# Where the causal mask of the attention scores is added: on TensorE before the score products, or on VectorE after them

## What is computed

```python
        s_own = jnp.einsum('bhqd,bhkd->bhqk', qf, k_own) * scale
        s_own = jnp.where(k_pos[None, :] <= q_pos[:, None], s_own, NEG)
        p = jax.nn.softmax(jnp.concatenate([s_sel, s_own], axis=-1), axis=-1)
```

## Time and profile before

| what | value |
|---|---|
| time, median of 3 runs | 826.17 us (826.13 to 826.72) |
| time of the profiled execution | 826.71 us |
| its span | 825.0 us |
| mean granted TensorE clock | 0.999 of 2.4 GHz |
| TensorE products busy | 815.7 us |
| VectorE busy | 612.4 us |
| ScalarE busy | 460.1 us |
| GpSimd busy | 153.2 us |

### The profile page before, as it was taken

One profiled execution on the slowest core, in us unless ns is written; L12 is line 12 of the kernel. 1 busy time (PEld: TensorE's weight loads), 2 busy tenths in 40 slices (PEclk: granted clock), 3 DMA queues, 4 the chain that ended last, 5 costly groups with the idle time before them and its releaser, 6 DMA issues.

```text
span 825.0 us, 12737 instructions
## 1 busy us (share of the span) xinstructions
PE 815.7 (99%) x4962; PEld 719.4 (87%) x4962; DVE 612.4 (74%) x734; ACT 460.1 (56%) x628; POOL 153.2 (19%) x146
## 2 busy tenths in 40 slices
PE   8999999999999999999999999999999999999997
PEld 8999888888989999999999988878899888888885
DVE  6899888977786766565787898888687767565664
ACT  6757687534664464545465577755355554445544
POOL 2407754082000000000000385523300000000000
PEclk9999999999999999999999999999999999999999
DMA  9976545567545555645567565465645465646451
GB/s 299 284 240 193 163 162 187 216 205 218 174 154 179 182 199 184 223 153 204 158 209 247 166 215 170 153 216 166 214 161 174 153 205 169 223 167 200 158 177 52
DMA packets 103598, 156.17 MB, mean 189 GB/s; under 512 B 4081, under 2 KB 68899, under 8 KB 103553
## 3 DMA queue, kind: packets, MB, share of 16 engines
q1 hardware_dynamic: 102080, 153.50, 56.5%
q0 software_dynamic: 1296, 1.79, 0.8%
q10 hardware_dynamic: 176, 0.27, 0.1%
HBM read 152.39 MB, written 1.05 MB: 186 GB/s over the span
## 4 chain that ended last, share of the span: by engine, by line
PE 93%; DVE 2%; ACT 2%; DMA 1%; issue 1%; DVEq 0%; ACTq 0%
PE bank L1093 19%; PE bank L1095 10%; PE bank L1038 8%; PE bank L1040 8%; PE bank L1039 8%; PE bank L981 7%; PE bank L982 7%; PE bank L983 7%; PE bank L1069 5%; PE bank L1070 5%; PE bank L1068 5%; ACT w_hi L648 1%; DMA raw<-in_w_in 1%; DVE w_lo L1445 1%; PE bank L1178 1%
## 5 line engine op out<-in xcount | busy, mean ns | idle before, releaser
L1445 DVE TENSOR_TENSOR w_lo<-raw,w_hi 128x2048 fp32r<-128x2048 f32 x135 | 318.6, 2361 | 133.1 <-ACT w_hi L648 132.4
L648 ACT ACTIVATE w_hi<-raw 128x2048 fp32r<-128x2048 f32 (+3 forms) x146 | 264.4, 1818 | 128.9 <-PE bank L1040 55.6
L1093 PE MATMUL bank<-act,w_hi 128*128 128x512 f32 x704 | 247.6, 395 | 0.0
L1095 PE MATMUL bank<-act,w_lo 128*128 128x256 f32 x704 | 197.0, 280 | 0.0
L1093 PEld LDWEIGHTS bank<-act,w_hi 128*128 128x128 f32 x704 | 132.0, 187 | 30.2
L1095 PEld LDWEIGHTS bank<-act,w_lo 128*128 128x128 f32 x704 | 132.9, 189 | 0.4
L1038 PE MATMUL bank<-w_hi,act 128*128 128x512 f32 x288 | 114.3, 397 | 0.0
L1040 PE MATMUL bank<-w_hi,act 128*128 128x512 f32 x288 | 112.3, 390 | 0.0
L1039 PE MATMUL bank<-w_lo,act 128*128 128x512 f32 x288 | 112.1, 389 | 0.0
L648 ACT ACTIVATE qk<-bank 128x256 f32<-128x256 f32 (+1 forms) x96 | 37.5, 395 | 76.4 <-PE bank L1095 76.3
L981 PE MATMUL bank<-act,w_hi 128*128 128x256 f32 x256 | 73.3, 286 | 1.2 <-DVE w_lo L1785 1.0
(11 more groups left out here) (250 smaller groups left out, 1453.0 us busy)
## 6 DMA issues: line engine op xcount, KB each, us to landing
raw<-in_w_ffn_in SPq DMA_DIRECT2D x44, 1024.0 KB, 5.1
raw<-in_w_gate SPq DMA_DIRECT2D x32, 1024.0 KB, 5.5
raw<-in_w_ffn_out SPq DMA_DIRECT2D x22, 1024.0 KB, 5.0
raw<-in_w_in SPq DMA_DIRECT2D x18, 1024.0 KB, 6.1
raw<-in_w_o SPq DMA_DIRECT2D x8, 1024.0 KB, 5.1
raw<-in_w_proj_b SPq DMA_DIRECT2D x4, 1024.0 KB, 4.9
raw<-in_w_in SPq DMA_DIRECT2D x12, 256.0 KB, 6.2
gates<-qk SPq DMA_DIRECT2D x32, 64.0 KB, 4.8
```

The costliest lines, as they stand in the source:

```text
L648: return nc.scalar.activation(o, i, ACT.Copy)
L1093: nc.tensor.matmul(bank[b + f], hi[:, k, fs], act2[:, k, :, :].rearrange("p h s -> p (h s)"), start=(k == 0), stop=False, skip_group_check ...
L1095: last = nc.tensor.matmul(main(b)[:, f, :], lo[:, k, fs], act_hi[:, k, :], start=False, stop=(k == KT - 1), skip_group_check=True)
L1445: V.tensor_tensor(w_lo[slot][:, :], raw[slot][:, :], w_hi[slot][:, :].bitcast(F32), ALU.subtract)\
```

## The change

The mask moves from TensorE to VectorE. TensorE's four mask products per pair go, and with them `ident16` and its copy on GpSimd; the first score product of each bank now starts the accumulation. `causal` becomes fp32. VectorE, once it has the scores, adds the mask in place in both banks and both diagonal blocks in one operation (2 banks x 2 blocks x 128 columns = 512 elements per partition, both the input and the output in PSUM, the mask read from SBUF for each of the four blocks) and waits for it with `link` before the reductions.

```diff
-DVE_CHAIN_PER_LAYER = 66
+DVE_CHAIN_PER_LAYER = 70
...
-        causal = sb("causal", [P, P], BF16)
-        ident16 = sb("ident16", [P, P], BF16)
+        causal = sb("causal", [P, P])
...
             pool.wait_ge(pre_const, 5)
-            nc.gpsimd.tensor_copy(ident16[:, :], ident[:, :])
-
...
                         bank_wait(l, 4 + i, f"S{hp}")
-                        nc.tensor.matmul(bank[4 + i][:, 0:P], ident16[:, :], causal[:, :], start=True, stop=False,
-                                         skip_group_check=True)
-                        nc.tensor.matmul(bank[4 + i][:, 2 * P:3 * P], ident16[:, :], causal[:, :], start=False,
-                                         stop=False, skip_group_check=True)
-
                     for i in range(2):
                         h = slice(64 * i, 64 * i + 64)
-                        nc.tensor.matmul(bank[4 + i][:, 0:P], qk[h, hp, 0:P], qk[h, 4 + hp, 0:P], start=False,
+                        nc.tensor.matmul(bank[4 + i][:, 0:P], qk[h, hp, 0:P], qk[h, 4 + hp, 0:P], start=True,
                                          stop=False, skip_group_check=True)
...
                     dve.wait_ge(s_done, l * 2 * HP + 2 * hp + 2)
+                    own = banks[:, 4:6, :].rearrange("p b (q k) -> p b q k", q=2)[:, :, :, 0:P]
+                    link(l, V.tensor_tensor(own, own, causal[:, :].unsqueeze(1).unsqueeze(1).to_broadcast([P, 2, 2, P]),
+                                            ALU.add))
                     V.tensor_reduce(mx[:, 0:2], banks[:, 4:6, 0:P], AX.X, ALU.max)
```

## The result

The changed kernel takes 831.25 us (median of 4, 829.70 to 832.43) against 826.34 us (826.13 to 826.72) beside it: the ratio is 1.0058, with a 95% interval of 1.0046 to 1.0070. It is slower by 4.9 us, where 1.5 us were forecast and 829.5 was the top of the range. The profiled execution took 829.70 us, span 828.0, so 3.0 us more than the profile of before. The 4.9 us are the sum of three parts: 3.0 us are in the profile, 1.5 us more lie between this execution, the fastest of the four, and their median, and 0.4 us between the profiled execution of before (826.71) and the median of its kernel.

What follows compares the result with a forecast made beforehand. TensorE was taken as the bound, but with nothing to spare at pair 3's probabilities, fed by VectorE's chain. These come 0.75 us later per layer; two layers, +1.5 on 826.17, gave 827.7 us, range 825.9 to 829.5.

Steps and rivals of the forecast that it cites:

- The gain of 0.24 per pair: TensorE's stream: of 0.33 us for the mask products, 0.09 stays as turning price; 0.24 saved per pair, 1.9 us in all.
- The place where it is lost: TensorE's transposes of pair 3 at unit 21: it waits about 1.7 us per layer for ScalarE's scaling of the probabilities.
- The price of the mask operation: VectorE's added operation: 0.69 us plus 0.04 for `link`, 0.73 per pair.
- The rival of a dear write to PSUM: VectorE's mask operation costs up to 1.11 us because it writes PSUM; 829.4 us, chance 0.18.
- `nmx` of pair 3 held by GpSimd's third tap: VectorE's `nmx` at pair 3 starts behind GpSimd's tap, takes near 0.68 us and ends 0.75 later than before.
- The rival of 826.7: Pair 3's `nmx` gets in before GpSimd's tap, takes 0.17 and ends 0.24 later per layer; 826.7 us, chance 0.12.
- The sum, pair 2 and pair 3: Chain through VectorE and ScalarE: exponentials move by -0.13 us at pair 2, probabilities of pair 3 by +0.75 per layer.
- All that follows on VectorE to the gates of unit 16 is +0.25: After pair 1's reduction moves by 0.73 - 0.48, VectorE's following tasks up to these gates all come 0.25 us later.
- its weak place: GpSimd's taps meet other VectorE operations; each meeting moves the chain up to 0.4 us either way, spread 826.9 to 828.7.
- Granted clock still 1.00 in both waits: Sign expected in the profile after: clock stays at 1.00 during TensorE's two waits of 1.7 us at pair 3.
- The rival that the gain is kept: TensorE keeps all eight savings of 0.24 us, with no loss at pair 3; 824.3 us, chance 0.10.

Runs made afterwards that it cites:

- the filler: Changed kernel with 36 products of zeros on TensorE in place of idling before pair 3's probabilities; 829.91 us, ratio 1.0035 against the kernel before.

## Why the prediction was wrong

- *The gain of 0.24 per pair*: right (0.32 in place of 0.56; 0.93 for the four pairs of a layer, 0.96 forecast).
- *The place where it is lost*: right. The only new wait is pair 3's transposes on ScalarE's scaling, twice. It is 2.4 long and not 1.7.
- *The price of the mask operation*, 0.69 and 0.04: right (0.70, and 0.03 to the reduction). The rival of a dear write to PSUM is out.
- *`nmx` of pair 3 held by GpSimd's third tap*: right (0.68, 0.68 forecast). The rival of 826.7 is out.
- *The sum, pair 2 and pair 3*: this step failed. "All that follows on VectorE to the gates of unit 16 is +0.25" took the tasks' durations as given. They aren't: between the pairs the chain lost 0.70 and 0.39 more, by meetings of VectorE's operations with GpSimd's taps. The prediction named this as its weak place, but put it as a spread around zero of up to 0.4 per meeting "either way"; in fact single meetings moved VectorE by 0.55, 0.38, 0.55 and 0.36, three of the four against it, and the term is 1.1 per layer. It was put at nothing without a reason: the only rows of GpSimd that the prediction works with are those of pair 3. 0.22 came back, since there was that much slack. So 1.60 per layer in place of 0.75, which makes 829.4 and would still have lain in the range, at its upper edge.
- *"Granted clock still 1.00 in both waits"*: this failed, and it is what put the median outside. The sum had no term for a wait that changes the clock. A fall measures 1.45 and 1.57 us, and the mean clocks speak for none to two falls per execution. With the filler the kernel is 3.3 us above the one before (829.91 against 826.60), as the 2 x 1.60 of the table has it; without, the median is 2.6 higher.
- *The rival that the gain is kept* is out for this kernel, but the gain is there to be had: with three taps at each of two pairs moved into VectorE's idle gaps, all of it is kept.

What stays open: why the clock falls behind one such wait and not behind the other, and from what length of wait on. With VectorE masking pair 3 alone TensorE waited 0.90 and all ten executions have mean clocks of 0.998 to 1.000. But one of ten executions without any mask (wait 0.22) has 0.996, and one of thirteen of before 0.997 at 830.18 us, so a lower mean clock is not unknown without a long wait.

## What to carry to other kernels

When the busiest engine is relieved, look for its wait with the least slack and follow what feeds it back to the engine whose program is full: behind its slack, the relief is worth only as much as that chain moves, and work added to the chain is paid in full. Such a chain can contain idle time of its own (here 2.06 us behind a wait for ScalarE); fill that first: here it turned a change that loses into one that gains. And when one engine moves by half a microsecond against another, operations of the two that meet can change their order and with it their durations (here by 0.36 to 0.55 each, 1.1 per layer), so a sum of unchanged durations has to be checked meeting by meeting before it is trusted.

## What the runs showed of the hardware

- A wait of TensorE of 1.9 to 2.4 us, in a stream that is otherwise full, is followed in some executions by 3.41 us at 1.2 GHz and in others, of the same program with the same wait, by nothing. A fall costs 1.45 to 1.57 us. With products of zeros in its place no execution of eight has a mean clock under 0.998.
- A waiting product starts 0.05 to 0.06 us after what it waited for (probabilities at 73.08, transpose at 73.13). In step with the stream it starts 0.23 after the product ahead; so the probabilities of before, ready 0.04 before the last product ahead began, had 0.22 of slack.
- An operation of VectorE with two SBUF inputs that starts while a tap of GpSimd has 0.68 us to run takes 0.55 longer (0.69 to 1.24, and 2.28 to 2.83); one that reads and writes PSUM beside a tap takes its usual 0.68 to 0.70.
- The whole stretch from pair 0 to pair 3 repeats to 0.02 us between layers and between executions (after: 73.13 and 73.14 us, and 73.12 and 73.14 in another execution), while whole executions differ by 1 us and more. The spans of the two profiles of the changed kernel are 2.1 apart: 0.65 of it lies in the opening and 1.45 in the clock.
